# Expert order worked out on the chip, with the first two items peeled off the loops

## The reference, cut to what matters

```
logits = t @ router_w + router_b                 # (256, 32)
top_val, top_idx = top_k(logits, 4); gates = softmax(top_val)
for every expert e, over the tokens that chose it:
    g, u = split(x_e @ w_gu[e] + b_gu[e])         # w_gu[e]: 1024 x 2048
    g = min(g, 7); u = clip(u, -7, 7)
    y = ((u + 1) * g * sigmoid(1.702 * g)) @ w_down[e] + b_down[e]   # w_down[e]: 1024 x 1024
    out[token] += gate * y
```

## Time and profile before

| | us |
|---|---|
| median of 3 runs | 1377.76 |
| lowest and highest | 1377.06, 1380.0 |
| the profiled execution | 1375.38 |
| its span | 1373.4 |

### The profile page before, as it was taken

One profiled execution on the slowest core, in us unless ns is written; L12 is line 12 of the kernel. 1 busy time (PEld: TensorE's weight loads), 2 busy tenths in 40 slices (PEclk: granted clock), 3 DMA queues, 4 the chain that ended last, 5 costly groups with the idle time before them and its releaser, 6 DMA issues.

```text
span 1373.4 us, 16150 instructions
## 1 busy us (share of the span) xinstructions
PE 1300.7 (95%) x5972; PEld 606.8 (44%) x5973; DVE 469.7 (34%) x928; ACT 186.7 (14%) x378; POOL 15.7 (1%) x48
## 2 busy tenths in 40 slices
PE   4999999999998999999999999999999996999997
PEld 2876876778843333333333333333333332333332
DVE  1020766333134333333323333233333432323333
ACT  2101322333011000100001000010001100001001
POOL 0000000110000000000000000000000000000000
PEclk9999999999998999999999999999999998999999
DMA  9746658225677999999999999999999999399993
GB/s 365 256 156 247 243 188 301 105 82 185 251 278 284 414 423 429 429 429 429 429 428 429 428 428 429 394 426 429 429 428 428 428 428 430 153 428 429 428 428 160
DMA packets 55982, 477.53 MB, mean 348 GB/s; under 512 B 4863, under 2 KB 4948, under 8 KB 28308
## 3 DMA queue, kind: packets, MB, share of 16 engines
q1 hardware_dynamic: 55652, 476.11, 84.2%
q10 hardware_dynamic: 304, 1.06, 0.2%
HBM read 476.10 MB, written 1.05 MB: 347 GB/s over the span
## 4 chain that ended last, share of the span: by engine, by line
PE 90%; DMA 5%; ACT 2%; DVE 1%; issue 1%; SPq 0%; DVEq 0%; ACTq 0%
PE bank L1482 31%; PE bank L1515 16%; PE bank L1200 12%; PE bank L1434 5%; PE bank L1471 4%; PE bank L1318 4%; PE bank L1191 4%; DMA down_ring<-in_w_down 4%; PE bank L1449 3%; PE bank L1381 2%; PE bank L1443 2%; DMA gu_ring<-in_w_ada 2%; ACT scratch L657 1%; PE bank L1460 1%; PE bank L1279 1%
## 5 line engine op out<-in xcount | busy, mean ns | idle before, releaser
L1482 PE MATMUL bank<-gu_ring,scratch 128*64 128x512 f32 x2048 | 460.5, 597 | 5.1 <-issue 3.7
L1482 PEld LDWEIGHTS bank<-gu_ring,scratch 128*64 128x64 f32 x2048 | 141.7, 137 | 289.1 <-issue 285.3
L1515 PE MATMUL bank<-down_ring,scratch 128*64 128x512 f32 x1024 | 227.4, 595 | 2.0 <-DMA down_ring<-in_w_down 2.0
L1200 PE MATMUL bank<-gu_ring 128*128 128x256 f32 x768 | 174.2, 385 | 2.1 <-ACT gu_ring L542 2.1
L1200 PEld LDWEIGHTS bank<-gu_ring 128*128 128x128 f32 x768 | 146.0, 193 | 25.3 <-issue 4.6
L1515 PEld LDWEIGHTS bank<-down_ring,scratch 128*64 128x64 f32 x1024 | 70.4, 137 | 134.7 <-issue 126.2
L1020 DVE TENSOR_TENSOR scratch<-bank,bgu 128x512 f32<-128x512 f32 x32 | 22.1, 692 | 280.5 <-PE bank L1449 280.5
L661 ACT ACTIVATE scratch<-bank 128x512 f32<-128x512 f32 x32 | 19.1, 597 | 704.4 <-PE bank L1482 704.4
L1002 DVE TENSOR_TENSOR xres<-xres,bank 128x512 f32<-128x512 f32 x132 | 81.8, 682 | 37.1 <-PE bank L1471 37.1
L1034 DVE TENSOR_TENSOR scratch<-bank,scratch 128x512 f32<-128x512 f32 x32 | 22.1, 692 | 182.1 <-PE bank L1515 182.1
L1434 PE MATMUL bank<-xn,onehot 128*64 128x512 f32 x264 | 72.7, 631 | 0.8 <-DVE onehot L955 0.8
(11 more groups left out here) (257 smaller groups left out, 778.0 us busy)
## 6 DMA issues: line engine op xcount, KB each, us to landing
gu_ring<-in_w_gu SPq DMA_DIRECT2D x128, 2048.0 KB, 21.4
down_ring<-in_w_down SPq DMA_DIRECT2D x64, 2048.0 KB, 14.5
gu_ring<-in_w_in SPq DMA_DIRECT2D x32, 1024.0 KB, 7.9
gu_ring<-in_w_ada SPq DMA_DIRECT2D x20, 1024.0 KB, 7.0
down_ring<-in_w_ada SPq DMA_DIRECT2D x4, 1024.0 KB, 10.1
gu_ring<-in_w_pa SPq DMA_DIRECT2D x4, 1024.0 KB, 6.3
gu_ring<-in_w_pb SPq DMA_DIRECT2D x4, 1024.0 KB, 6.1
gu_ring<-in_w_o SPq DMA_DIRECT2D x4, 1024.0 KB, 10.3
```

Source lines behind the costliest of these rows:

```text
L1200: last = M(dst[:, b * T:(b + 1) * T], group_chunk(group, kt // 4)[:, kt % 4, cols], hT[:, kt, :], start=kt == 0, stop=kt == KT - 1)
L1482: last = M(bank[f // 2][64 * a:64 * a + 64, :], xT[:, kt % 4, kt // 4, :], gu_ring[:, 8 * half + kt, f * 512:(f + 1) * 512], start=kt == 0 ...
L1515: last = M(bank[7][64 * a:64 * a + 64, :], act_sb[:, kt % 4, kt // 4, :], down_ring[:, kt // 2, (kt % 2) * D + a * 512:(kt % 2) * D + (a + ...
```

## The change

Items 0, 1 and 2 stay experts 0, 1 and 2. The other experts follow an order that is worked out on the chip during item 0: an expert with index 3 or more that has further passes is *late*. Late experts get the items from 16 on (`LATE`), in order of their index; the others fill the remaining items in order. The order stands in a small tile `order` of three rows: expert of an item, its count of further passes, and the number of further passes before it. From item 2 on the engines read it: SP, for the address of each load; DVE, for the columns of `gated`, `onehot` and bias; and PE, ACT and DVE for the counts. Items 0 and 1 are written out ahead of the loops on PE, ACT and DVE. SP, ACT and DVE wait for the order before their loops, PE inside item 0.

```
+FIXED = 3
+LATE = NE // 2
+        def expert_at(eng, item, most=NE - 1):
+            return eng.value_load(order[0:1, 0, bass.ds(item, 1)], min_val=0, max_val=most)
+        def further_passes(eng, counts, first, one_pass):
+            count = eng.value_load(counts, min_val=0, max_val=FURTHER_BLOCKS)
             with eng.If(count > 0):
+                before_it = eng.value_load(first, min_val=0, max_val=T * TOPK // FCAP)
...
+        def passes_of_expert(expert):
+            return passes[0:1, 0, expert:expert + 1], passes[0:1, 1, expert:expert + 1]
+        def passes_at(item):
+            return order[0:1, 1, bass.ds(item, 1)], order[0:1, 2, bass.ds(item, 1)]
@@ SP
+            load_item_gu(2, 0, 2)
+            load_item_down(1, 1)
+            sp.wait_ge(order_ready, 1)
             with sp.Fori(1, TOGETHER // 2) as n:
+                load_item_gu(n * 2 + 1, 1, expert_at(sp, n * 2 + 1))
+                load_item_down(n * 2, expert_at(sp, n * 2))
+                load_item_gu(n * 2 + 2, 0, expert_at(sp, n * 2 + 2))
+                load_item_down(n * 2 + 1, expert_at(sp, n * 2 + 1))
...
             with sp.Fori(TOGETHER // 2 + 1, PAIRS) as n:
                 for half in range(2):
+                    expert = expert_at(sp, n * 2 + half)
+                    load_item_gu(n * 2 + half, half, expert)
+                    load_item_down(n * 2 + half, expert)
@@ ACT
+            for n in range(2):
+                further_passes(act, *passes_of_expert(n), further)
+                expert(n)
+            act.wait_ge(order_ready, 1)
+            with act.Fori(2, NE) as n:
+                further_passes(act, *passes_at(n), further)
                 expert(n)
@@ DVE
+            def place_experts():
+                frank, late = bank[3][0:NE, 0:1], bank[3][0:NE, 1:2]
+                is_late, moved, pos, alt, col = (place[:, n:n + 1] for n in range(5))
+                V.scalar_tensor_tensor(is_late, expert_no[0:NE, :], float(FIXED), over[:, 0:1], op0=ALU.is_ge, op1=ALU.mult
+                                       ).then_inc(late_ready, 1)
+                dve.wait_ge(late_counted, 1)
+                own.then(V.tensor_tensor(pos, expert_no[0:NE, :], frank, ALU.subtract))
+                own.then(V.scalar_tensor_tensor(moved, pos, float(LATE), late, op0=ALU.is_ge, op1=ALU.mult))
+                own.then(V.tensor_tensor(pos, pos, moved, ALU.add))
+                own.then(V.scalar_tensor_tensor(alt, frank, float(LATE), pos, op0=ALU.add, op1=ALU.subtract))
+                own.then(V.scalar_tensor_tensor(col, alt, is_late, pos, op0=ALU.mult, op1=ALU.add))
+                V.tensor_scalar(at_place[:], iota[0:NE, 0:NE], -1.0, col, ALU.add, ALU.is_equal).then_inc(place_ready, 1)
+                V.memset(order_f[:, :, NE:NE + 1], float(NE))
+                dve.wait_ge(order_done, 1)
+                own.then(V.tensor_copy(order_f[:, 0:2, 0:NE], bank[3][0:1, 64:64 + 2 * NE].rearrange("p (a e) -> p a e", a=2)))
+                own.then(V.tensor_tensor_scan(order_f[:, 2, 0:NE], order_f[:, 1, 0:NE], ones[0:1, 0:NE], 0.0,
+                                              op0=ALU.add, op1=ALU.mult))
+                own.then(V.tensor_tensor(order_f[:, 2, 0:NE], order_f[:, 2, 0:NE], order_f[:, 1, 0:NE], ALU.subtract))
+                V.tensor_copy(order[:], order_f[:]).then_inc(order_ready, 1)
+            def expert(item, this, following, first_one=False):
...
+                pick(following)
+                if first_one:
+                    place_experts()
                 add_given(item - 1)
...
+            dve.wait_ge(order_ready, 1)
+            with dve.Fori(2, NE) as n:
+                own.start_at(n * PER + (start + PLACES))
+                this, following = expert_at(dve, n), expert_at(dve, n + 1, NE)
+                further_passes(dve, *passes_at(n), lambda b, k: further(n, this, b, k))
+                expert(n, this, following)
@@ PE, expert(item, half, fills, first_one=False)
                     if kt == 1:
+                        if first_one:
+                            pe.wait_ge(late_ready, 1)
+                            M(bank[3][0:NE, 0:1], before[0:NE, 0:NE], place[:, 0:1], start=True, stop=True)
+                            M(bank[3][0:NE, 1:2], ones[0:NE, 0:NE], place[:, 0:1], start=True, stop=True).then_inc(late_counted, 1)
                         give(item - 1)
+                    if kt == 4 and first_one:
+                        pe.wait_ge(place_ready, 1)
+                        M(bank[3][0:1, 64:64 + NE], expert_no[0:NE, :], at_place[:], start=True, stop=True)
+                        M(bank[3][0:1, 64 + NE:64 + 2 * NE], over[:, FURTHER_BLOCKS:FURTHER_BLOCKS + 1], at_place[:],
+                          start=True, stop=True).then_inc(order_done, 1)
+                if first_one:
+                    pe.wait_ge(order_ready, 1)
                 gate_up(KT - 2, (2, 3))
...
+            for half in range(2):
+                further_passes(pe, *passes_of_expert(half), lambda b, k: further(half, half, 1, k))
+                expert(half, half, 1, first_one=half == 0)
+            with pe.Fori(1, PAIRS) as n:
```

More of the change, by code:

```diff
@@ L182, in build @@
         passes = sb("passes", [1, 2, NE], I32)
+        expert_no = sb("expert_no", [P, 1])
+        place = sb("place", [NE, 5])
+        at_place = sb("at_place", [NE, NE])
+        order_f = sb("order_f", [1, 3, NE + 1])
+        order = sb("order", [1, 3, NE + 1], I32)
         small = sb("small", [P, 8])
@@ L683, in _ @@
             nc.scalar.preload_act_table(ACT.Sigmoid)
-            with act.Fori(0, NE) as n:
-                further_passes(act, n, further)
+            for n in range(2):
[4 more added lines that the diff above has]
+                further_passes(act, *passes_at(n), further)
                 expert(n)
@@ L1003, in add_given @@
                                     ).then_inc(given_added, 1)
-            def expert(item):
-                bias = bgu[:, bass.ds(item, 1), :].rearrange("p e r -> p (e r)")
+            def place_experts():
[17 more added lines that the diff above has]
+                V.tensor_copy(order[:], order_f[:]).then_inc(order_ready, 1)
+            PLACES = 8
+            def expert(item, this, following, first_one=False):
+                bias = bgu[:, bass.ds(this, 1), :].rearrange("p e r -> p (e r)")
                 dve.wait_ge(back_ready, item + 1)
@@ L1010, in expert @@
                     for a in range(2):
-                        last = V.tensor_scalar(gated[:, tt, a, :], iota[:], r1[:, tt, bass.ds(item, 1)],
-                                               gates[:, tt, bass.ds(item, 1)], ALU.is_equal, ALU.mult)
+                        last = V.tensor_scalar(gated[:, tt, a, :], iota[:], r1[:, tt, bass.ds(this, 1)],
+                                               gates[:, tt, bass.ds(this, 1)], ALU.is_equal, ALU.mult)
                         if 2 * tt + a < 3:
@@ L1015, in expert @@
                 last.then_inc(gated_ready, 1)
-                pick(item + 1)
+                pick(following)
+                if first_one:
+                    place_experts()
                 add_given(item - 1)
@@ L1037, in _, with further @@
             FURTHER = 1 + 1 + 1 + 1 + 1
-            def further(expert, b, k):
+            def further(item, expert, b, k):
                 f = further_own
@@ L1058, in further @@
                 dve.wait_ge(f_onehot, k * 2 + 2)
-                dve.wait_ge(back_ready, expert + 1)
+                dve.wait_ge(back_ready, item + 1)
                 for tt in range(TT):
@@ L1090, in _ @@
             V.memset(small[:, 7:8], 0.0).then_inc(f_mark, 1)
-            with dve.Fori(0, NE) as n:
-                own.start_at(n * PER + start)
-                further_passes(dve, n, lambda b, k: further(n, b, k))
-                expert(n)
+            for n in range(2):
+                places = PLACES if n else 0
+                own.start_at(n * PER + places + start)
+                further_passes(dve, *passes_of_expert(n), lambda b, k: further(n, n, b, k))
+                expert(n, n, n + 1, first_one=n == 0)
+                assert own.steps == PER + (0 if n else PLACES)
+            dve.wait_ge(order_ready, 1)
[4 more added lines that the diff above has]
+                expert(n, this, following)
                 assert own.steps == PER
@@ L1472, in give, with expert @@
                       ).then_inc(given_done, 1)
-            def expert(item, half, fills):
+            def expert(item, half, fills, first_one=False):
                 pe.wait_ge(xTe_ready, item + 1)
@@ L1585, in _ @@
             pe.wait_ge(passes_ready, 1)
-            with pe.Fori(0, PAIRS) as n:
+            for half in range(2):
+                further_passes(pe, *passes_of_expert(half), lambda b, k: further(half, half, 1, k))
+                expert(half, half, 1, first_one=half == 0)
+            with pe.Fori(1, PAIRS) as n:
                 for half in range(2):
```

(2 more changed lines are left out.)

32 lines of the change are left out of this document (14 added, 18 removed).

## The result

| | before | after |
|---|---|---|
| median | 1378.0 us (1377.1 to 1380.0) | 1389.6 us (1384.4 to 1391.1) |
| ratio, 95% interval | | 1.0070 [1.0052, 1.0087] |
| profiled execution | 1375.4 us, span 1373.4 | 1391.1 us, span 1388.9 |

Slower, by 11.6 us on the medians where 6.4 were forecast, and above the range; the interval of the ratio means 7.2 to 12.0 us. In another set of runs the same changed kernel had 1387.4 us against 1379.8, ratio 1.0051 [1.0031, 1.0072], or 4.3 to 9.9 us, which takes in the forecast.

What follows compares the result with a forecast made beforehand. The weight stream, slower than PE, was taken as the bound, with PE living on a shrinking reserve of loaded weights. Terms 4.7 + 1.0 + 0.7 = +6.4 us on 1377.8 gave 1384.2 us, range 1379.0 to 1387.6.

Steps and rivals of the forecast that it cites:

- the term for the written-out items: Extra code copies of items 0 and 1: four more code packets, taken as 0, up to 4.5 us.
- the two stalls stay: PE's waits for weights in the second down halves of items 14 and 15, 1.02 and 0.98 us, remain.
- DVE's loads: Two more register loads per item on DVE, uncovered only ahead of the further pass: +1.0 us, from 0 to 1.4.
- The main term: Weight reserve after the pass, moved to item 16, ends at item 27; the last four items wait: +4.7 us.
- the prediction's own sign: Main term wrong if no gate/up waits in the last four items, or if stalls of items 14 and 15 are gone.
- rival (c): Branches of items 0 to 3: code is fetched in the open, +4.5 us more, 1388.7 us; chance 0.08.
- PE's delay goes into the total: Item 0: the stream is waiting for PE there, so PE's planning delay counts in full, +0.7 us.
- Item 0's planning: Small products and DVE steps working out the order in item 0: +0.7 us, from 0.3 to 2.0.
- rival (b): Further pass is cheaper at its new place through a faster clock, 5.1 us saved, 1379.1 us; chance 0.08.
- Idle for about 30 us: After the further pass the DMA engines are idle once, with 29.6 us of nothing to load.
- Rival (a): Weight stream after the pass keeps up with PE, the reserve lasts: 1379.5 us, no change; chance 0.10.
- (d): Order comes out as it was, expert 25 not counted as late: +1.7 us, 1379.5 us; chance 0.04.

Runs made afterwards that it cites:

- the order alone: Kernel before with the new order written down at build time, expert 25 as item 16, no planning, register loads or written-out items: 1385.2 us, ratio 1.0042 [1.0028, 1.0055].

## Why the prediction was wrong, point by point

The main mechanism was right and its size too; the step that failed is the term for the written-out items, put at 0, and with it the statement that the two stalls stay. Together they are worth 1.4 to 3.7 us by the ledger and 1.9 on the medians of their own experiment. That alone can account for what the second set has over the forecast (7.7 against 6.4), but not for the 5.2 us in the first set. DVE's loads add 0.5; what is left of the first set's is not placed. The clock in the pass, which differs between executions, may be part of it.

- **The main term was right.** "The reserve ends at item 27, and the last four wait", +4.7. The last pair of gate/up 18 landed at 954.1 + 25.3 = 979.4 and was wanted at 983.9 + 7.0 = 990.9, a reserve of 11.5 (11.4 foretold). Items 28 to 31 cost 4.9; moving the pass by 2 and by 9 items took away two waits and all four; the order alone has them all. By the prediction's own sign ("or if the stalls of items 14 and 15 are gone") the main term would be wrong; the sign was badly chosen. The stalls go with the written-out items and no new order, and stay with the new order and nothing written out: they tell of another term.
- **The step that failed: "I take 0" for the written-out items.** They cost 6.3 us in one profile and 4.0 in the other (3.7 and 1.4 less the stalls that went), by the mechanism of rival (c), in two places rather than four and with more each: the price is not the transfer's 1.1 us but 2.3 to 2.8 us from the packet's start to going on, less what PE still has queued, and at times a slow restart. Rival (c)'s 1388.7 lies near the first median, but by luck: it adds four transfers and leaves out the stalls that went. I took the loop as the nearest row; the nearest row was the first turn of the loop, where four packets had come and were hidden behind queued products. That a request was hidden at one place says nothing for the next. The prediction did give a bound, "up to 4 x 1.1 = 4.5 us", but left it out of "with all bounds"; with it the range would have reached 1387.6 + 4.5 = 1392.1 and taken in the result.
- **"The two stalls of items 14 and 15 lie ahead of it and stay" failed with it.** They went, 2.6 us, because PE came later and the stream did not lose as much. That also limits "PE's delay goes into the total": true only so long as nobody downstream was waiting for the stream. In the set of runs that measured the changed kernel with and without written-out items together, the net was none.
- **DVE's register loads:** +1.0 foretold, 1.4 to 1.6 measured (4.4 against 3.0 and 2.8), at or just over its upper bound.
- **Item 0's planning:** +0.7 foretold, 0.4 between the first two profiles. Item 0's down projection comes 1.9 later still in the changed kernel's other profile, but 1.6 and 2.3 later than in before also in the two kernels with nothing but written-out items, so the start can't tell the planning's cost. Within item 0 it is 0.55: 21.85 us from the first gate/up product to the down projection, against 21.30. `is_late` came in time. The four small products took 0.15 + 0.06 us a pair where I had taken 0.37.
- **What the forecast did not have:** the clock in the pass. I weighed it only as a gain, rival (b), and took the pass of the one profile (10 us at 1.2 GHz) as what a pass costs. It was a cheap one: of the four traces with the pass at item 25, the other three have 17 us. That the times of four of the changed kernel's executions meet the forecast of 1384.2 is the other side of the same chance.
- **"Idle for about 30 us"** was 36.1: the item with the pass was 6.7 us longer than in before.
- **The sum by the terms as measured:** 4.9 + 1.5 + 0.4 + (1.4 to 3.7) = 8.2 to 10.5, against medians 11.6 and, in the other set, 7.7 above before, and 7.8 +- 0.9 at equal clock. Rival (a) and (d) are refuted by the four waits, (b) by the order alone.

## What to carry to other kernels

Where a ring of weights is filled a little more slowly than it is used, a pause of the consumer is worth only what it refills, and one that comes while the ring is full is thrown away: put it where the reserve has just run out, and count the items behind it. New code is priced at its first visit: ask what the engine still has queued when it leaves a block of code, and expect the answer, and the item in which it falls due, to change with every shift of the code. A lost microsecond upstream of a stream-bound stretch is partly given back; look there before you add it to the total.

## What the runs showed that I had not expected

- After a packet of code that starts at the end of PE's queued work, PE goes on 2.3 to 2.8 us later (twelve cases, with the DMA engines at 414 to 427 GB/s from 460 to 560 us). Some 160 instructions ahead of the code made it cost nothing; some 80 moved one of the stand-stills to item 0. A loop that has turned once fetched no more, though a branch skips a part of it in every item.
- A gap of 2 us can leave the products behind it at the lower clock (5.35 us for 16, against 3.43), and another of 3.1 us did not (3.65).
- The same kernel's item with the further pass cost 37.2 and 40.3 us over an ordinary one in two executions, by its clock; two profiles are no measure of a pass with waits in it.
